# Summing a group's squares on VectorE before the all-ones product, in the state-space stage of a hybrid decoder trunk

## What is computed

```python
y = y.reshape(b, s, SSM_D_INNER) * jax.nn.silu(z.astype(jnp.float32))
yg = y.reshape(b, s, SSM_GROUPS, SSM_D_INNER // SSM_GROUPS)
yg = yg * lax.rsqrt(jnp.mean(yg * yg, axis=-1, keepdims=True) + NORM_EPS)
```

## Time and profile before

| | us |
|---|---|
| median of 3 runs | 1912.97 (1912.83 to 1913.38) |
| profiled execution, its own time | 1913.2 |
| its span, first to last instruction | 1911.3 |
| TensorE busy | 1886.4 (99%) |
| VectorE busy | 1174.2 (61%) |
| ScalarE busy | 924.2 (48%) |
| mean granted TensorE clock | 0.996 |

### The profile page before, as it was taken

The page is one execution under the profiler, slowest core; times in us unless marked ns, Lnnn a source line. Parts: engine busy times, 40 slices in busy tenths (PEclk is TensorE's granted clock), DMA queues, the critical chain, the costliest instruction groups (busy, mean ns, idle before and its releaser), DMA issues.

```text
span 1911.3 us, 27093 instructions
## 1 busy us (share of the span) xinstructions
PE 1886.4 (99%) x9554; PEld 1598.5 (84%) x9554; DVE 1174.2 (61%) x1351; ACT 924.2 (48%) x1074; POOL 68.5 (4%) x105
## 2 busy tenths in 40 slices
PE   8999999999999999999999999999999999999997
PEld 7888888888888888888888888888888888888885
DVE  6655555565656888875555576556555655565674
ACT  5545444545345555564444464334434443444563
POOL 2010000000000100000000000100000000000010
PEclk9999999999999999999999999999999999999998
DMA  6665555666565655555566566656665565556553
GB/s 228 208 232 176 176 176 176 210 217 190 194 192 184 204 172 187 184 173 194 187 208 196 171 201 222 194 186 193 192 196 187 187 197 189 185 186 199 175 185 124
DMA packets 99950, 364.62 MB, mean 191 GB/s; under 512 B 11545, under 2 KB 11689, under 8 KB 99465
## 3 DMA queue, kind: packets, MB, share of 16 engines
q1 hardware_dynamic: 96624, 351.32, 56.9%
q0 software_dynamic: 2960, 12.36, 1.9%
q10 hardware_dynamic: 304, 0.12, 0.0%
HBM read 361.60 MB, written 3.70 MB: 191 GB/s over the span
## 4 chain that ended last, share of the span: by engine, by line
PE 92%; DVE 4%; ACT 2%; issue 1%; DMA 1%; DVEq 0%; SPq 0%; ACTq 0%
PE ps L1401 26%; PE ps L1423 17%; PE ps L1424 17%; PE ps L1425 17%; PE ps L1405 13%; DVE w_lo L678 1%; ACT w_hi L317 1%; DMA w_raw<-w_stream 1%; DVE xs L875 0%; PE ps L1579 0%; DVE x_sq L725 0%; DVE x_tok L1276 0%; DVE xdt L1034 0%; PE ps L1581 0%; PE ps L1600 0%
## 5 line engine op out<-in xcount | busy, mean ns | idle before, releaser
L678 DVE TENSOR_TENSOR w_lo<-w_raw,w_hi 128x1024 fp32r<-128x1024 f32 x662 | 820.2, 1245 | 591.4 <-ACT w_hi L317 588.5
L317 ACT ACTIVATE w_hi<-w_raw 128x1024 fp32r<-128x1024 f32 x662 | 693.4, 1057 | 696.4 <-PE ps L1425 482.7
L1401 PE MATMUL ps<-act,w_hi 128*128 128x512 f32 x2320 | 734.0, 397 | 1.2 <-DVE act L1121 1.0
L1423 PE MATMUL ps<-w_hi,act 128*128 128x512 f32 x1344 | 525.9, 391 | 2.0 <-DVE act L1121 1.6
L1424 PE MATMUL ps<-w_lo,act 128*128 128x512 f32 x1344 | 523.9, 390 | 0.0
L1425 PE MATMUL ps<-w_hi,act 128*128 128x512 f32 x1344 | 523.7, 390 | 0.0
L1405 PEld LDWEIGHTS ps<-act,w_lo 128*128 128x128 f32 x2320 | 435.8, 188 | 102.0
L1405 PE MATMUL ps<-act,w_lo 128*128 128x256 f32 x2320 | 457.4, 278 | 0.0
L1401 PEld LDWEIGHTS ps<-act,w_hi 128*128 128x128 f32 x2320 | 355.0, 189 | 4.7 <-issue 2.2
L1423 PEld LDWEIGHTS ps<-w_hi,act 128*128 128x128 f32 x1344 | 252.8, 188 | 56.3 <-DVE w_lo L678 2.1
L1425 PEld LDWEIGHTS ps<-w_hi,act 128*128 128x128 f32 x1344 | 252.8, 188 | 52.9
(11 more groups left out here) (217 smaller groups left out, 842.8 us busy)
## 6 DMA issues: line engine op xcount, KB each, us to landing
w_raw<-w_stream SPq DMA_DIRECT2D x662, 512.0 KB, 4.1
a_rows<-decay_rows POOLq DMA_DIRECT2D x8, 512.0 KB, 5.7
x_T<-x_in SPq DMA_DIRECT2D x4, 512.0 KB, 8.0
x_tok<-x_tok_in POOLq DMA_DIRECT2D x4, 512.0 KB, 5.7
out<-x_tok SPq DMA_DIRECT2D x3, 512.0 KB, 2.8
bias<-bias_rows POOLq DMA_DIRECT2D x8, 128.0 KB, 3.2
gain_mix<-gains_in POOLq DMA_DIRECT2D x1, 1024.0 KB, 6.0
gain_mlp<-gains_in POOLq DMA_DIRECT2D x1, 1024.0 KB, 6.5
```

Source lines behind the costliest of these rows:

```text
L317: act.activation(whi[:, s, :], raw[:, s, :], ACT.Copy).then_inc(hi_ready, 1)
L678: dve.tensor_tensor(wlo[:, s, :], raw[:, s, :], whi[:, s, :], ALU.subtract)\
L1401: pe.matmul(bank[2 * g + t], whi[:, s, at_:at_ + P], a.rearrange("p a t -> p (a t)"), start=first and i == 0, stop=False)
L1423: pe.matmul(out_, hi, whi[:, s, n], start=first and i == 0, stop=False)
```

## The change

In the VectorE program a new `group_squares` adds tiles 2 and 3 of `group_sq` onto tiles 0 and 1 (128x512), and then tile 1 onto tile 0 (128x256). The second add waits for the first by a new semaphore, `squares_added`. Both stand at c = 0 of the next group, after that step's `split_lo` and ahead of the first taps; for the last group they stand after `split_lo` at c = 0 of `gm`. TensorE's `sum_group` waits for `squares_added` in place of `group_squared` and runs one product in place of four.

```diff
@@ VectorE
+            def group_squares(g):
+                dve.wait_ge(group_squared, g + 1)
+                dve.tensor_tensor(group_sq[:, 0:2, :], group_sq[:, 0:2, :], group_sq[:, 2:4, :], ALU.add)\
+                   .then_inc(squares_added, 1)
+                dve.wait_ge(squares_added, g * 2 + 1)
+                dve.tensor_tensor(group_sq[:, 0, :], group_sq[:, 0, :], group_sq[:, 1, :], ALU.add)\
+                   .then_inc(squares_added, 1)
...
             def group(g, first=False, last=False):
                 for c in range(16):
                     step(g * 16, U + c)
+                    if c == 0 and not first:
+                        group_squares(g - 1)
                     if c == 0:
                         dve.wait_ge(block_done, g * 4 + B)
...
             for c in range(56):
                 step(0, U + c)
+                if c == 0:
+                    group_squares(GROUPS - 1)
                 if c == 1:
                     group_variance(GROUPS - 1)
@@ TensorE
             def sum_group(g):
-                pe.wait_ge(group_squared, g + 1)
-                for t in range(4):
-                    mm = pe.matmul(bank[4][:, 0:T], ones[:, :], group_sq[:, t, :], start=t == 0, stop=t == 3)
-                mm.then_inc(group_summed, 1)
+                pe.wait_ge(squares_added, g * 2 + 2)
+                pe.matmul(bank[4][:, 0:T], ones[:, :], group_sq[:, 0, :], start=True, stop=True)\
+                    .then_inc(group_summed, 1)
```

More of the change, by code:

```diff
@@ L256, in build @@
         group_squared, group_summed = sem("group_squared"), sem("group_summed")
+        squares_added = sem("squares_added")
         group_var, group_std_ready, group_rs = sem("group_var"), sem("group_std_ready"), sem("group_rs")
```

## The result

The changed kernel takes 1917.11 us, the median of 19 runs (1915.54 to 1918.36), against 1912.83 for 19 runs of the kernel before (1911.71 to 1913.57). The ratio is 1.0022, with a 95% interval of 1.0016 to 1.0028: slower by 4.3 us. The span of its profiled execution is 1914.9 us, 3.6 more than before. Its runs also spread more widely: standard deviation 0.79 us against 0.54.

A forecast was written before the change was run, and what follows sets the result against it. VectorE's chain up to `xdt`, then TensorE's units, was taken to bound groups 1 to 3, and TensorE alone `gm`. The terms 1.54 + 0.89 + 1.32 = +3.75 us gave 1916.7 us, range 1914.6 to 1918.2.

The forecast's parts named there:

- The bound: Groups 1 to 3: VectorE's chain up to `xdt`, then TensorE's units, set the length; at `gm` TensorE alone.
- VectorE's chain: From split to first tap, the adds lengthen it by 0.77 us in groups 1 and 2 each, 0.89 in group 3.
- the rows of x_sq: At the kernel's start, same-shaped VectorE adds: 0.76 us each for 128x512 when waited for, 0.61 without a wait.
- The 0.10 that I added for the loop: In the loop of groups 1 and 2, waiting for VectorE's own result costs 0.10 us more: 2.33 instead of 2.23.
- TensorE's wait: At each sum TensorE idles some 2.2 us for the adds; covered in groups 1 to 3, +1.32 us at `gm`.
- The waits for `xdt`: At c = 11 they shorten by about 0.4 us in groups 1 and 2, about 0.2 in group 3.
- Rival B: TensorE's clock falls in the new idle times: 3.0 us at `gm`, 1919.7; all four, more than 1925; chance 6%.
- The sum: Over groups 1 to 3 and `gm`: 1.54 + 0.89 + 1.32 = +3.75 us, forecast 1916.7 us.
- the low case at `gm`: Adds follow each other at 0.61 us and the loop adds nothing: 1.07 us, in a low sum of 2.85.
- The rule of the Trainium skill: A semaphore between chained VectorE instructions costs nothing extra; the sum would be about 0.6 us smaller, 1916.1 us.
- A: VectorE's idle times of 1.44 and 1.25 us soak the adds up: +1.6 us, 1914.6 us; chance 8%.
- C: TensorE never waits for the adds: only `gm` gains, 1911.7 us, or all 5.2 us, 1907.8; chance 2%.

The follow-up runs named there:

- the adds alone: Against the kernel before: VectorE does both adds into a spare tile nothing reads, TensorE keeps four products and its old wait; 1915.15 us, ratio 1.0013.
- The doubled adds with filling: The change with both adds done twice, and thirteen useless products ahead of TensorE's wait; 1920.74 us, ratio 1.0043 against the kernel before.
- the filled change: The change with eight useless all-ones products on TensorE ahead of its wait for the adds; 1916.13 us, ratio 1.0018 against the kernel before.
- the filled kernels: Useless products put ahead of TensorE's wait: eight in the change, 1916.13 us; thirteen in the change with both adds done twice, 1920.74 us.
- the kernel with the last sum only: The change for the last group's sum alone, groups 0 to 2 keeping four products and no adds; 1914.67 us, ratio 1.0011 against the kernel before.
- the doubled adds: The change with both adds done twice, first into a spare tile nothing reads; 1924.04 us, ratio 1.0058 against the kernel before.
- the kernel with the later product: The change with the one product moved behind TensorE's next unit, c = 1 for c = 0; 1913.74 us, ratio 1.0006 against the kernel before.

## Why the prediction was right, and where it was not

**The bound.** Held. Sparing TensorE 5.2 us gained 1.0, expected 1.3, and left the length of the groups at 52.15; delaying VectorE alone lengthened each.

**VectorE's chain.** Forecast +0.77, +0.77 and +0.89; the adds alone gave +0.71, +0.70 and, from split to `xdt` in group 3, 34.86 against 33.99, +0.87. The second add starts 0.71 behind the first, where the rows of x_sq had led me to 0.76. The 0.10 that I added for the loop is there, but in another gap: 0.44 us from the second add to the first tap in groups 1 and 2, 0.34 in group 3.

**TensorE's wait.** Forecast product at 689.30 with a split at 686.83, so 2.47 behind it; measured 688.78 - 686.44 = 2.34. At `gm` +1.32 was forecast, +1.30 came. The doubled adds with filling tested the whole sum at about twice the size: 8.3 expected, 8.1 measured.

**The waits for `xdt`.** This step of what the profile would show was wrong for groups 1 and 2. I had said that their wait would shorten by 0.4; in group 1 it stayed at 1.11. TensorE had two waits there, 0.28 for `w_lo` and 1.10 for `xdt`, and I charged its lateness of 1.21 against both when I asked whether it is covered, but against the second alone when I said what would be seen. The wait for `w_lo` went first. The trace gives the rest: counted from the split, TensorE came to unit c = 10 later than before by 1.09 us, of which the gone wait took 0.27 and the longer first pair behind that wait 0.11, which leaves 0.71, just VectorE's own 0.71, and so the wait for `xdt` stayed as it was. In group 3, which has only one, the shortening of 0.2 came as stated (0.79 to 0.56).

**Rival B** was right in kind and wrong in size. I gave 6% to falls of the clock, at 3 us each, as a case apart. They are part of the ordinary execution of this change: one in the first profile, two in the second, and none in the stage in the kernels without the new idle time. I had priced a fall from the one behind the longest idle time of the trace. The working was wrong: a mean of 0.71 over six microseconds is a loss of 6 x 0.29 = 1.7 us, not the 3 of six microseconds at half rate. That the whole fall did cost some 3.2 us there (0.50 from 31 to 37 us, 0.75 to 38) was not in the row. Behind 2.1 to 2.3 us of idle time it is half as long and costs 1.6 us, of which 0.4 counts in groups 1 and 2, 0.95 in group 3 and all at `gm`.

**The sum.** Without falls the fixed points give 0.71 + 0.70 + 0.87 + 1.30 = 3.58 us, and the filled change measured +3.5. The forecast of 3.75 is 0.17 above that, mostly the 0.76 for the first add that is 0.71, and it has no term for the falls. The two errors point in opposite ways, so that 3.75 comes so near to the measured 4.3 is in part luck. The interval of the measurement, 3.1 to 5.4, holds all of these. The falls are also what widens the spread, as the granted clocks of the runs show. The change came out at 1.0022, with the 0.2% on which the forecast stood inside its interval. One bound was off as well: by its own terms the low case at `gm` is 1.32 - 0.15 = 1.17 and not 1.07, so the low sum is 2.95; the range does not hang on it.

**The rule of the Trainium skill** in "VectorE: DVE Perf Modes", section "The DRAIN you can't avoid", gave a sum of 3.1 us, since a semaphore between chained instructions is said to cost nothing. With the wait the adds start 0.71 us apart; an instruction that did not wait for the add before it came 0.61 behind the earlier trace rows. So the rule is nearer than I had it and still not met here. On the clock, the Trainium skill's "TensorE: Matmul & The Clock Gate", section "What's actually happening", says that activity releases the throttle: the filled kernels agree, since work of no use kept the clock at 2.4 GHz.

**Rivals A and C** fell: idle times of VectorE that hang on its own earlier work stayed at 1.43 and 1.26, and TensorE never found the adds done.

## What to carry to other kernels

Before moving work from a busy engine to a less busy one, find which engine's chain sets the length of that stage: here the engine with 61% did, and the one with 99% merely waited less. Where the work must go on such a chain, look for a pause that ends with somebody else's result and put it there; the same two adds cost 4.6 us more behind the split than ahead of it. A wait that stops TensorE costs its length and sometimes a slower clock behind it, so move the product behind the next block of work rather than let it stand first in line; here that took the change from +3.7 or +4.3 to +1.1.

## What the runs showed of the hardware that was not expected

TensorE's granted clock can fall behind an idle time of only 2.1 to 2.3 us, but need not: three falls behind eight such sums in the two profiles of the change, one behind the one such sum in the kernel with the last sum only, three behind four idle times of 3.3 to 3.5 us in the doubled adds, none behind the waits of 1.1 us or, in the kernel with the later product, of 1.67. In the one at `gm` a step took 1.27 us in place of 0.69 and the loss was 1.6 us. In the change and the last-sum kernel the clock fell up to 1.4 us after TensorE had started again. Idle times of 0.3 to 0.6 us with filler products before them showed none. What decides whether a given idle time brings a fall is open.

GpSimd's adds lengthened VectorE's instructions beside them, a 128x1024 split from 1.22 to 1.48 us and four taps from 1.38 to 1.59. GpSimd's own 128x256 add took 1.59 us beside VectorE and 0.74 at `gm`, where VectorE was idle; its 128x512 add was not slower beside VectorE (1.29 against 1.38).
